# Down projection in groups of two features behind every chunk, in a two-layer streaming encoder

## What is computed

```python
def conv_ffn(h, prev, w_gate, w_up, conv_w, conv_b, w_down):
    t = h.shape[1]
    g = h @ w_gate
    gp = jnp.concatenate([prev.astype(g.dtype), g], axis=1)
    c = conv_b
    for j in range(CONV_W):
        c = c + conv_w[j] * gp[:, j:j + t]
    y = (jax.nn.gelu(c) * (h @ w_up)) @ w_down
    return y, gp[:, t:]
```

## Time and profile before

| | us |
|---|---|
| median of 3 runs | 2043.69 (2041.55 to 2044.95) |
| profiled execution | 2041.2 |
| its span, first to last instruction | 2039.4 |
| TensorE busy | 1981.2 |
| VectorE busy | 1245.1 |
| ScalarE busy | 816.9 |
| GpSimd busy | 422.4 |
| first MLP, chunk 0 to the first matmul of the last group | 597.7 to 1025.9 |
| second MLP, likewise | 1577.9 to 2004.3 |

### The profile page before, as it was taken

The page is one execution under the profiler, slowest core; times in us unless marked ns, Lnnn a source line. Parts: engine busy times, 40 slices in busy tenths (PEclk is TensorE's granted clock), DMA queues, the critical chain, the costliest instruction groups (busy, mean ns, idle before and its releaser), DMA issues. The chain is left out here.

```text
span 2039.4 us, 30005 instructions
## 1 busy us (share of the span) xinstructions
PE 1981.2 (97%) x11870; PEld 1719.3 (84%) x11870; DVE 1245.1 (61%) x2086; ACT 816.9 (40%) x1324; POOL 422.4 (21%) x590
## 2 busy tenths in 40 slices
PE   9999989999998999999999999999999899999998
PEld 7889768987788888989889888799777898988986
DVE  5453664435468867677753467653454977768784
ACT  4222553435354433233344446243534533424342
POOL 3012121000133313224110123210012322322311
PEclk9999999999999999999999999999999999999999
DMA  5324143245645446446221211723484554545441
GB/s 177 126 68 162 53 166 130 93 149 183 257 94 133 99 114 157 92 114 145 94 79 63 83 43 47 255 81 123 174 312 97 114 124 114 135 114 124 93 146 56
DMA packets 161052, 254.01 MB, mean 125 GB/s; under 512 B 9123, under 2 KB 99535, under 8 KB 160846
## 3 DMA queue, kind: packets, MB, share of 16 engines
q1 hardware_dynamic: 91234, 148.00, 21.3%
q0 software_dynamic: 69680, 104.08, 21.1%
HBM read 235.11 MB, written 18.24 MB: 124 GB/s over the span
## 5 line engine op out<-in xcount | busy, mean ns | idle before, releaser
L2332 DVE TENSOR_TENSOR w_lo<-raw,w_hi 128x1024 fp32r<-128x1024 f32 x177 | 213.0, 1218 | 235.1 <-ACT w_hi L1714 231.8
L897 PE MATMUL bank<-w_hi,hT_lo 128*128 128x512 f32 x720 | 290.1, 403 | 2.8 <-DVE w_lo L2332 1.4
L899 PE MATMUL bank<-w_hi,hT_hi 128*128 128x512 f32 x720 | 281.4, 391 | 0.0
L898 PE MATMUL bank<-w_lo,hT_hi 128*128 128x512 f32 x720 | 280.6, 390 | 0.0
L897 PE MATMUL bank<-hT_hi,w_lo 128*128 128x320 f32 (+2 forms) x800 | 249.2, 311 | 5.8 <-DVE af L2869 4.5
L899 PE MATMUL bank<-hT_hi,w_hi 128*128 128x320 f32 (+2 forms) x800 | 247.2, 309 | 0.0
L898 PE MATMUL bank<-hT_lo,w_hi 128*128 128x320 f32 (+2 forms) x800 | 247.1, 309 | 0.0
L1714 ACT ACTIVATE w_hi<-raw 128x1024 fp32r<-128x1024 f32 x177 | 182.6, 1051 | 152.8 <-DMA raw<-w_ffn_down 75.8
L1711 ACT ACTIVATE w_hi<-raw 128x1024 fp32r<-128x1024 f32 x132 | 137.0, 1053 | 256.7 <-DMA raw<-w_ffn_up 123.1
L2324 DVE TENSOR_TENSOR w_lo<-raw,w_hi 128x1024 fp32r<-128x1024 f32 x132 | 160.2, 1219 | 67.7 <-ACT w_hi L1711 67.5
L2405 DVE TENSOR_TENSOR x<-x,bank 128x512 f32<-128x512 f32 x160 | 109.5, 684 | 128.7 <-PE bank L899 128.1
(11 more groups left out here) (440 smaller groups left out, 4150.9 us busy)
## 6 DMA issues: line engine op xcount, KB each, us to landing
raw<-w_ffn_gate SPq DMA_DIRECT2D x44, 512.0 KB, 5.3
raw<-w_ffn_up SPq DMA_DIRECT2D x44, 512.0 KB, 7.0
raw<-w_ffn_down SPq DMA_DIRECT2D x22, 1024.0 KB, 6.6
kcX<-cache_mem_k POOLq DMA_DIRECT2D x16, 1024.0 KB, 7.0
vcX<-cache_mem_v POOLq DMA_DIRECT2D x16, 1024.0 KB, 6.8
raw<-w_in_even SPq DMA_DIRECT2D x13, 1024.0 KB, 5.4
raw<-w_in_odd SPq DMA_DIRECT2D x12, 1024.0 KB, 5.2
sumN<-w_ffn_gate POOLq DMA_DIRECT2D x40, 256.0 KB, 4.0
```

Of the source, the lines that this page charges most:

```text
L897: pe.matmul(out, wl, xh, start=first, stop=False)
L898: pe.matmul(out, wh, xl, start=False, stop=False)
L899: return pe.matmul(out, wh, xh, start=False, stop=last)
L2332: dve.tensor_tensor(w_lo[:, s, 0:n], raw[:, q % 2, UNIT * i:UNIT * i + n], flat(w_hi[:, s, 0:n]), ALU.subtract).then_inc(*lo_made.mark(c, u))
```

## The change

Groups have two features and follow every chunk from the second on, except that the last two chunks stand together and the last group has four features (ten groups for six). VectorE and ScalarE gate the first feature of a chunk beside the group that follows it and the second inside the next chunk. Between two chunks without a group, both features are gated in the second of them. Beside a group, some additions to x stand ahead of the next weight units. At the start of an MLP two bank copies (`c11`), a weight half and the sum of the gate move forward. SyncE's load q waits, where load q-2 was the first half of a chunk, for the sum that makes S4 and the low half of S3 instead of the low half of S4. The diff, cut:

```diff
-GROUPS = (FT + FG - 1) // FG
-SHORT = FT - FG * (GROUPS - 1)
+GROUPS = FT // 2 - 1
...
+def group_size(g):
+    return 4 if g == GROUPS - 1 else 2
...
 FFN_PLAN = [("gu", 0), ("gu", 1), ("dn", 0)]
 for _g in range(1, GROUPS - 2):
-    FFN_PLAN += [("gu", 2 * _g), ("gu", 2 * _g + 1), ("dn", _g)]
-FFN_PLAN += [("gu", FT // 2 - 3), ("gu", FT // 2 - 2), ("gu", FT // 2 - 1), ("dn", GROUPS - 2), ("dn", GROUPS - 1)]
+    FFN_PLAN += [("gu", _g + 1), ("dn", _g)]
+FFN_PLAN += [("gu", FT // 2 - 2), ("gu", FT // 2 - 1), ("dn", GROUPS - 2), ("dn", GROUPS - 1)]
...
@@ SyncE
-                    sp.wait_ge(*lo_made.at(oc, PARTS.index("A22" if ou else "S4") if oc[0] == "gu" else ou + on - 1))
+                    if oc[0] == "gu" and ou == 0:
+                        sp.wait_ge(*dve_done.at("sum", oc, "S4"))
+                        sp.wait_ge(*lo_made.at(oc, PARTS.index("S3")))
+                    else:
+                        sp.wait_ge(*lo_made.at(oc, PARTS.index("A22") if oc[0] == "gu" else ou + on - 1))
...
@@ VectorE, down(g, f)
                             if f is not None:
-                                if (t, n) == (0, 0):
-                                    taps(f + 1)
                                 if (t, n) == (0, 1):
                                     gated(f)
                                 if (t, n) == (1, 0):
                                     low_a(f)
-                                    if g:
-                                        refill_lo(FIRST_UNIT[c] + 4)
-                                if (t, n) == (1, 1):
-                                    gated(f + 1)
-                                if (t, n) == (2, 0):
-                                    low_a(f + 1)
+                                if g and (t, n) in ((1, 1), (2, 1)):
+                                    refill_lo(FIRST_UNIT[c] + 2 + t)
+                                if g == GROUPS - 2:
...
@@ VectorE, the walk through the plan
+                c11(0, "g")
+                c11(0, "u")
+                refill_lo(FIRST_UNIT[("gu", l, 0)] + 4)
+                low_t("t3", t3[0][:, :, :], t3[1][:, :, :], t3F[:, :, :], 0)
+                to_sums(0, "g")
                 fourth_sum(("gu", l, 0))
...
                     refill_lo(g0 + 6)
-                    to_sums(i, "g")
+                    if i:
+                        taps(2 * i - 1)
+                        to_sums(i, "g")
...
                     to_sums(i, "u")
-                    if i == 0:
+                    if i:
+                        gated(2 * i - 1)
+                        low_a(2 * i - 1)
+                    else:
                         low_t("n4", n4[0][:, :, :], n4[1][:, :, :], hF[:, 1, :, 0:HT], 0)
```

More of the change, by code:

```diff
@@ L149, in units_of @@
     if c[0] == "dn":
-        return FG if c[2] else SHORT
+        return group_size(c[2])
     if c[0] == "gu":
@@ L2751, in down @@
                         for n in range(2):
[L2752 to L2755 removed]
+                            if g == 0 and t == T - 1 and n == 1:
+                                refill_lo(FIRST_UNIT[c] + 4)
+                            if behind and t == T - 1 and n == 1:
                                 split_lo(NEXT[c], [1, 2, 3])
                             if f is not None:
[L2758 to L2759 removed]
                                 if (t, n) == (0, 1):
@@ L2763, in down @@
                                     low_a(f)
-                                    if g:
-                                        refill_lo(FIRST_UNIT[c] + 4)
-                                if (t, n) == (1, 1):
-                                    gated(f + 1)
-                                if (t, n) == (2, 0):
-                                    low_a(f + 1)
+                                if g and (t, n) in ((1, 1), (2, 1)):
+                                    refill_lo(FIRST_UNIT[c] + 2 + t)
+                                if g == GROUPS - 2:
+                                    if (t, n) == (0, 0):
+                                        taps(f + 1)
+                                    if (t, n) == (1, 1):
+                                        gated(f + 1)
+                                    if (t, n) == (2, 0):
+                                        low_a(f + 1)
                                 if (t, n) == (3, 0) and g == 0:
@@ L2784, in down @@
                     if g < GROUPS - 1:
-                        for k in range(2 if g else 1, units_of(c)):
+                        for k in range(1, units_of(c)):
                             refill_lo(FIRST_UNIT[c] + 4 + k)
@@ L2849, in second_tokens @@
                     else:
+                        if f >= 2:
+                            dve.wait_ge(*dve_done.at("a", l, f - 2))
                         dve.tensor_tensor(af[e][:, HT:TOK], one[:, 0:HT], two[:, 0:HT], ALU.subtract).then_inc(*signal)
```

70 lines of the change are left out of this document (29 added, 41 removed).

## The result

The changed kernel takes **1997.99 us** (1997.12 to 1998.46, 4 runs) for 2043.39 us (2041.55 to 2044.95) of the kernel before in the same comparison: ratio 0.9778, 95% interval 0.9761 to 0.9795. The profiled execution took 1997.77 us (span 1996.0), 43.4 us less than the profiled one before.

The account below looks back on a forecast made before the run. TensorE, busy 1981.2 of 2039.4 us, was taken as the bound, losing time to a late VectorE. Terms -38.9 + 4.8 - 4.6 = -38.7 us from 2041.2 give 2002.5, plus 2.5 for the median: 2005 us, range 1999 to 2021.

Parts of the forecast that it names:

- The stretch from the third chunk on: Third chunk to end of fifth group, each FFN: TensorE's lost 17.8 and 17.4 us go, with VectorE keeping up.
- The residue, +4.8: Later pairs of chunk and group: 0.3 us lost in each of 16, +4.8 us, bounds 0 and 32.
- Why VectorE is late: Chunk following a chunk: VectorE gates both predecessor features before emptying its own banks, though busy only 253.92 of 348.61 us.
- Part 2: SyncE's load of the group's weights: issued near 4.4 us into the chunk, wanted near 16.7, slowest landing 9.9, so hidden.
- The start, -4.6: Start of each FFN: earlier bank copies save 2.6 to 3.3 us in the first, 1.4 to 2.1 in the second.
- The wait of 4.4 us: First chunk of an FFN: TensorE waits 4.4 us before S4 of the gate for the up branch's sum.
- chunk 1's wait of 0.8 us: Second chunk of an FFN: waits about 0.8 us for an S1 sum.
- From the profiled execution to the median, +2.5: Whole kernel: median of the runs 2.5 us above the profiled execution, taking 2002.5 to 2005 us.
- A: Groups of two: each loses 1.7 to 2.0 us, sixteen times, time near 2031; chance 0.10 shared with the start-only rival.
- B: Next chunk's second weight half lands late: above 11.1 us it costs every period, 2055 us at 14.5; chance 0.05.
- C: Small groups put TensorE to its lower clock: 18 groups take some 10 us more each, near 2195 us; chance 0.01.
- D: Only the FFN start is mended, VectorE waiting for ScalarE instead: 2036 us; chance 0.10 shared with the small-groups waits rival.

Follow-up runs that it names:

- experiment 6: Kernel before with results ahead of weight units' low halves and SyncE's changed wait: 2008.33 us; that order alone 2032.10 us, the load's wait alone 2008.00 us.
- experiment 4: Changed kernel with repeated low halves on VectorE ahead of the fourth addition beside each group from the second on: two repeats 2015.52 us, four 2063.26 us.

## Why the prediction was right and where it was wrong

**The stretch from the third chunk on: right.** 17.8 and 17.4 us were to go, 18.0 and 17.6 went; the first group was to lose 2.0 and 1.7 us less and loses 2.03 and 1.79 less. The period laid out by hand was met closely: A22's half at T+10, the S1 sum of the gate at T+13.5, the group's units at T+21.6, where I had 9.9, 13.3 and 21.4; the first addition was done at T+26.8, as laid out. VectorE's work in the stretch came to 282.8 us, where I had 275.8 to 281.3: the four groups there became eight, so all 40 of the new additions fall into it, not 32 of them. Such a table of two engines is worth the work.

**The residue, +4.8: wrong, it is 0. This is the step that failed.** I took 0.3 us per period from the chunk of 24.92 us, because it was the nearest row in place. I had not asked what that row waited for. The trace of before has the answer, on VectorE in that chunk:

```profile
1673.98 1.23 DVE L2324 TENSOR_TENSOR w_lo<-raw,w_hi 128x1024 fp32r<-128x1024 f32 x1 [5.63 <-ACT w_hi L1711]
...
1675.58 0.48 DVE L2855 TENSOR_TENSOR u2g<-u2g,bank 128x320 f32<-128x320 f32 x1
```

A22's second bank opens at 1676.12 for 1675.9, as soon as this result is there. It is a late load with results behind it. The order alone and the load's wait alone each bring this chunk to 24.6 us (24.59 and 24.61, experiment 6), and the change has both. A bound from a row is only as good as the cause behind it.

**"Why VectorE is late": wrong, and right by luck.** The waits stood at the bank copies behind the gating, and I named what stood ahead of them. The cause was a chunk earlier, an idle VectorE: 5.6 us for a high half. I had read the list of TensorE's waits and VectorE's busy time but not VectorE's own waits. The gating was not innocent: it stands ahead of the low half for which the load waits, and about 9 us remain when the load alone is mended. As the change moves both the gating and the load, the wrong cause gave the right sum; for the kernel of experiment 6 it would have given 2026 to 2037 for 2008.

**Part 2, SyncE's load "hidden": true of the new kernel, and the wrong question.** I asked whether the new wait costs something, not what the old one had cost. Alone it is worth 35 us.

**The start, -4.6: mis-sized, -3.3.** The wait of 4.4 us was right (4.16), and chunk 1's wait of 0.8 us did not come. But the clock, which I had put at little, did cost something: in the wait, 0.6 us before its end in the first MLP and 1.7 in the second, the granted clock falls to 0.5, for 3.4 us in the first and 6.7 in the second. TensorE from the end of the first of these waits on:

```profile
623.13 0.61 PE L898 MATMUL bank<-hT_hi,w_lo 128*128 128x320 f32 x1 [4.16 <-DVE p1u L2834]
624.07 0.47 PE L898 MATMUL bank<-hT_hi,w_lo 128*128 128x320 f32 x1
...
626.25 0.31 PE L898 MATMUL bank<-hT_hi,w_lo 128*128 128x320 f32 x1
```

S4 takes 1.4 us more in the first MLP and 2.4 in the second, and with chunk 1 no longer waiting, nothing makes up for it. Chunks 0 and 1 are 2.8 and 0.6 us shorter than before.

**From the profiled execution to the median, +2.5: wrong, +0.2.** I carried the difference between one profiled execution and a median of three over to another kernel; it was scatter.

Together: 4.8 + 2.3 - 1.3, and 1.2 that the stretch, the first groups and the rest of the program gave beyond my terms, make the 7.0 us between 2005 and 1998. Residue and offset both leaned to the slow side: without them the forecast would have been 1997.7, below the 1999 at which the range began, although my own lower bound for the residue was 0.

**The rivals.** A (waits move into the small groups) does not occur, but it is what happens as soon as a second gating (14.7 us groups), two weight units (15.1) or 2.5 us of work (14.4) stand there. B (a late transfer) does not occur and was the right thing to fear: the load at T+13.7 instead of T+4.6 makes 2051 us of 1998. C (a lower clock in small groups): 1.00 over both stretches. D (only the start is mended) does not occur; the 2036 that I wrote for it does not follow from my terms either, since 2043.7 less the 4.6 of the start is 2039.

## What to carry to other kernels

Where an engine that is idle a quarter of the time is always late, read that engine's own waits before you blame what stands ahead of the late instruction: a unit that waits for a transfer holds up every result queued behind it on that engine. Look next at the signal on which the transfer's issue waits, and use the earliest one that is sound; here that was five lines for 35 us, while ten groups for six, with forty more additions in each MLP, were worth nothing that could be measured. A bound taken from a row needs the row's cause: if the change removes that cause, the bound is 0.

## What the runs showed of the hardware

- Landing changed with what else was under way: the first 1 MB load of chunk 5 took 8.2 us behind GpSimd's transfers and 5.0 us ahead of them; the median of all down loads went from 6.6 to 5.0 us with no byte less.
- Waits of 1.6 us left TensorE's granted clock at 1.00; in those of 2.8, 4.2 and 5.9 us at the start of an MLP it fell to 0.5. With four repeats (experiment 4) it fell just behind a wait of 2.21 us (ended at 707.4) and not at one of 2.23 (ended at 749.7). The slow time at the same wait of 4.2 us was 3.4 or 6.7 us; which of the two MLPs had the longer one changed from kernel to kernel. Why is open.
- Two VectorE instructions (low halves, 128x1024) that each wait for the one before take 2.52 us until the next starts; unlinked ones of the same size follow each other every 1.14.
